# Conditioning products moved from the second router head into the latent turns, and eight expert loads moved with them

## The reference

```python
mod = jax.nn.silu(c) @ w_ada + b_ada            # w_ada: 1024 x 6144
sh1, sc1, ga1, sh2, sc2, ga2 = jnp.split(mod, 6, axis=-1)
h = modulate(rms_norm_2(x, g_attn), sh1, sc1)
x = x + ga1[:, None, :] * hybrid_mixer(h, w_in, b_f, sinks, w_out)
h2 = modulate(rms_norm_2(x, g_mlp), sh2, sc2)
x = x + ga2[:, None, :] * conv_glu_mlp(h2, w_up, conv_w, conv_b, w_down)
return rms_norm_2(x, g_final)
```

## Time and profile before

| | |
|---|---|
| Median of 3 runs | 1623.3 us (1623.09 to 1624.7) |
| The profiled execution | 1624.69 us |
| Its span, first to last instruction | 1622.8 us |
| TensorE, VectorE, ScalarE, POOL busy | 84%, 35%, 16%, 6% of the span |
| Mean granted clock of TensorE | 0.93 |
| Read from HBM | 510.6 MB, 315 GB/s over the span |
| Experts of layer 1: block 0's first product; last block's down products | 786.5 us; 1229.3 to 1233 us |

### The profile page before, as it was taken

How to read it: one execution, slowest core, us unless ns; L and a number is a source line. 1 busy time by engine, 2 the same in 40 slices (tenths; PEclk the granted TensorE clock), 3 DMA queues, 4 the chain that set the end, 5 groups by cost and what they waited for, 6 DMA issues and landing times.

```text
span 1622.8 us, 24320 instructions
## 1 busy us (share of the span) xinstructions
PE 1366.1 (84%) x9358; PEld 827.5 (51%) x9358; DVE 564.2 (35%) x1487; ACT 263.5 (16%) x736; POOL 103.7 (6%) x191
## 2 busy tenths in 40 slices
PE   8999999676776777989998766767767999999998
PEld 4445555343443443555554433433434875888843
DVE  3444543122122222562542221221213143577721
ACT  2144211010010011452111010100101133111100
POOL 1312000000000001210100000000001041000000
PEclk9999999898898898999998888988989979999999
DMA  8868999999999999636999999999999621544400
GB/s 285 310 234 302 370 392 419 421 421 422 422 421 422 422 421 397 225 132 226 380 408 422 420 422 422 422 422 422 422 421 367 231 78 52 195 152 149 141 0 26
DMA packets 117188, 512.76 MB, mean 316 GB/s; under 512 B 11856, under 2 KB 46604, under 8 KB 64888
## 3 DMA queue, kind: packets, MB, share of 16 engines
q1 hardware_dynamic: 115504, 507.56, 79.1%
q0 software_dynamic: 1584, 4.13, 0.8%
q10 hardware_dynamic: 24, 0.02, 0.0%
HBM read 510.61 MB, written 1.07 MB: 315 GB/s over the span
## 4 chain that ended last, share of the span: by engine, by line
PE 34%; DMA 12%; SPq 7%; DVE 2%; issue 1%; ACT 1%; POOL 0%; POOLq 0%; DVEq 0%; ACTq 0%
PE bank L2170 9%; DMA ring<-in_moe_w_up 7%; SPq L1618 6%; PE bank L2185 5%; PE bank L1218 4%; DMA BC<-in_moe_w_up 3%; PE bank L1914 3%; DMA ring<-in_moe_w_down 2%; PE bank L404 2%; PE bank L416 2%; PE bank L1204 1%; PE bank L1233 1%; PE bank L644 1%; PE bank L667 1%; PE bank L501 1%
## 5 line engine op out<-in xcount | busy, mean ns | idle before, releaser
L1218 PE MATMUL bank<-ring,hT 128*32 128x256 f32 (+1 forms) x2912 | 301.4, 462 | 156.2 <-DMA ring<-in_moe_w_up 68.9
L1218 PEld LDWEIGHTS bank<-ring,hT 128*32 128x32 f32 (+1 forms) x2912 | 157.1, 133 | 265.3 <-issue 178.9
L1218 PE MATMUL bank<-BC,hT 128*32 128x256 f32 (+1 forms) x1120 | 164.9, 463 | 48.2 <-DMA ring<-in_moe_w_up 28.2
L1469 DVE TENSOR_SCALAR pT<-pT 128x256 f32<-128x256 f32 x34 | 10.0, 294 | 462.7 <-ACT pT L1585 462.7
L2170 PE MATMUL bank<-hT,ring 128*128 128x256 f32 (+1 forms) x736 | 154.3, 373 | 1.7 <-ACT hT L294 1.7
L2170 PEld LDWEIGHTS bank<-hT,ring 128*128 128x128 f32 x736 | 136.4, 193 | 19.2 <-DVE hT L299 1.9
L501 PE MATMUL bank<-ring,hT 128*128 128x512 f32 (+4 forms) x352 | 123.7, 513 | 9.7 <-DVE hT L297 3.9
L1204 PE MATMUL bank<-A,hn 128*128 128x128 f32 x1088 | 128.1, 276 | 0.0
L1204 PEld LDWEIGHTS bank<-A,hn 128*128 128x128 f32 x1088 | 125.3, 193 | 3.3 <-issue 3.3
L1218 PEld LDWEIGHTS bank<-BC,hT 128*32 128x32 f32 (+1 forms) x1120 | 82.2, 135 | 86.2 <-issue 72.9
L1233 PE MATMUL bank<-ring,gtab 128*32 128x512 f32 (+1 forms) x800 | 123.6, 595 | 2.4 <-DMA ring<-in_moe_w_down 1.9
(11 more groups left out here) (297 smaller groups left out, 1489.7 us busy)
## 6 DMA issues: line engine op xcount, KB each, us to landing
ring<-in_moe_w_down SPq DMA_DIRECT2D x100, 1024.0 KB, 26.3
ring<-in_moe_w_up SPq DMA_DIRECT2D x94, 1024.0 KB, 26.5
ring<-in_moe_w_gate SPq DMA_DIRECT2D x88, 1024.0 KB, 25.3
BC<-in_moe_w_gate SPq DMA_DIRECT2D x36, 1024.0 KB, 25.0
BC<-in_moe_w_up SPq DMA_DIRECT2D x34, 1024.0 KB, 25.9
BC<-in_moe_w_down SPq DMA_DIRECT2D x28, 1024.0 KB, 26.9
ring<-in_w_ada SPq DMA_DIRECT2D x24, 1024.0 KB, 6.4
ring<-in_w_up SPq DMA_DIRECT2D x22, 1024.0 KB, 5.3
```

The lines of the kernel that those rows point to most:

```text
L1218: i = nc.tensor.matmul(GATE[q * cap:(q + 1) * cap, part * FF:(part + 1) * FF], xg[:, c, q * cap:(q + 1) * cap], u[:, c, :], start=(c == 0) ...
```

## The change

`cond3` is planned ahead of `o2` (8 conditioning units, then 4 of the output weights) and uses bank 3. Its products leave the router head: units 0 and 1 stand after `pkv` and ahead of `t4q`, behind a wait for `pkv`'s last copy; units 2 to 4 stand behind fills 1, 3 and 5 of `t4q`, units 5 to 7 behind fills 1, 3 and 5 of `t4k`. ScalarE copies and stores between `t4k` and the attention. Expert units 7 to 14 now follow the conditioning units in their slots, and SyncE loads them right after units 0 and 1; 15 to 18 follow the output weights. In the router head a `KeepWarm` filler issues one product of 512 columns of constants, into bank 1, at each of the eight places; nothing reads it, and its copy and its wait are empty.

```diff
-        def turn_stage(name, ready, jobs, scalar_only=False, fill_ready=None, bank0=4):
+        def turn_stage(name, ready, jobs, scalar_only=False, fill_ready=None, bank0=4, beside=None):
...
                     i.then_inc(turned.sem, 1)
+                    if beside:
+                        beside(pe, f)
...
+        class KeepWarm:
+            def tensor(self, pe, h):
+                nc.tensor.matmul(bank[1][:, :], ident, konst[:, P:P + NB], start=True, stop=True)
+            def bank_read(self, pe):
+                pass
+            def scalar(self, act, h):
+                pass
...
                 for m in range(EXTRA, 18):
-                    load_fixed(m)
+                    if m not in [early for early, _ in slots_free]:
+                        load_fixed(m)
...
-        t4q = l_turn("t4q", q_l, 0, scalar_only=True)
-        t4k = l_turn("t4k", k_l, 1, bank0=6)
+        def condition_first(pe):
+            pe.wait_ge(*pkv.copied(8))
+            cond3.tensor(pe, 0)
+            cond3.tensor(pe, 1)
+
+        def condition(first):
+            def beside(pe, f):
+                if f % 2 and f < 6:
+                    cond3.tensor(pe, first + f // 2)
+            return beside
+        t4q = l_turn("t4q", q_l, 0, scalar_only=True, beside=condition(2))
+        t4k = l_turn("t4k", k_l, 1, bank0=6, beside=condition(5))
...
+        cond3 = Conditioning(2, 3, 8, 3)
         o2 = OutStage(square_units(t["mla_w_out"][0], D, order="(c p)"), add_x)
         a2 = attention_stage("a2", l_turned, [latent_head(h) for h in range(HEADS)], MLA_QK ** -0.5, causal_bias, o2)
-        cond3 = Conditioning(2, 3, 8, 1)
...
         m2 = moe(1, "m2", o2.ready, a2.ready, rows_turned,
-                 [(3, first_half_2), (5, first_half_2), (4, second_half_2), (6, second_half_2)], cond3, lambda pool: conditioning_gpsimd(pool))
+                 [(m, rows_turned) for m in range(7, 15)] +
+                 [(3, first_half_2), (5, first_half_2), (4, second_half_2), (6, second_half_2)], KeepWarm(), lambda pool: conditioning_gpsimd(pool))
...
             t4k.scalar(act)
+            cond3.scalar(act, 7)
             a2.scalar(act)
...
             pkv.tensor(pe)
+            condition_first(pe)
             t4q.tensor(pe)
```

## The result

The changed kernel takes 1626.64 us (median of 20 executions, 1624.46 to 1631.05), the kernel before, timed beside it, 1624.5 us (20 executions, 1619.7 to 1626.75). The ratio is 1.0020, 95% interval 1.0011 to 1.0028: about 3.3 us slower (1.8 to 4.5); the two medians differ by 2.1. That is a small loss, clear of zero, and near the edge of the band of 0.2% within which the prediction had put it.

A forecast was written before the change was run, and what follows sets the result against it. Weight transfers were taken to bound about 880 to 1229 us, engines the time before. Terms +1.7, +0.5 and -0.5 summed to +1.7 us: 1625.0 from the median, 1626.4 from the profiled execution; given as 1625.2, range 1621.5 to 1628.5.

The forecast's parts named there:

- What bounds it: Second layer: engines set the time until about 880 us, then weight transfers; the queue is empty near 787 and 805 us.
- rival A: Expert loads during the attention: the early load pays, up to 19.9 us off, 1603 to 1619 us; chance 0.07.
- The conditioning products: Between the query and key turns: TensorE alone sets the pace, scores start at 712.48 us; +1.7 us.
- rival E: In the turns: a unit costs its lone price of 1.06 us as the array drains; +3.1, 1626.4 us; chance 0.08.
- The row I held against it: Old router head: the next work began 0.88 us after a lone unit, counted against a lone price of 1.06.
- The rule on small tiles: In the turns: less than full overlap of column tiles would make a unit 1.1 us and the term +3.5.
- ScalarE's copy and store: Before the attention's first exponential: it starts 0.54 us later, as does the first turned map; +0.5 us (0 to 0.7).
- The stand-ins: Router head: length kept, but TensorE's clock may change; full clock makes it 1.05 us shorter; counted -0.5 us (-1.05 to 0).
- I count half: Router head: half of the 1.05 us saved at full clock was counted, giving -0.5 us.
- POOL's small loads: Eight small conditioning and bias loads move from 800 us into the idle head; 0 us, bound -0.6.
- Rival C: In the turns: TensorE falls to half clock between 699 and 711 us, costing 1.85 us; 1627.3 us; chance 0.18.
- Rival B: Router head keeps full clock, 1.05 us off, and later falls move too; net +0.5 to +1.2, 1624 us; chance 0.2.

## Why the prediction was right, and where its sum was off

**What bounds it: right.** The byte count said that the queue is empty at 787 and at 805 us. In the changed kernel it stands idle 17 us earlier, and with the loads put back it is empty at 790 us all the same. The early load is worth nothing that can be measured (rival A), shown by the kernel that lacks it.

**The conditioning products: mis-sized, 1.7 us forecast, 3.24 measured.** The step that failed is the sum 8 x 0.88 + 16 x 0.445 = 14.16 us of work in one string. The shape was right: TensorE is the pace from the last copy to the last fill and waits for nobody. The lengths were right too (0.88 in the string of eight, 0.87 a pair). What was missing is a price for each change between the units' column tiles and the whole array: a pair of fills 0.87 among its like and 1.03 ahead of a unit, a unit 0.88 and 1.00 ahead of a pair. From 695.08 to the end of the issue of the last fills, near 710.8, it is 15.7 us, 1.6 more than the sum; with 0.87 a pair it is 1.8 more, 13 changes at about 0.14. A part of it, some 0.05 at each return to the fills, is also paid behind a wait: a pair's row is 1.09 long behind a wait or a unit and 1.04 straight behind the key/value products. That is rival E, to which I gave 0.08. Its +3.1 was the better number for the string, though half of the price lies on the fills and not on the unit. That the array drains at a change was its reason; the runs show the price and not what happens inside. Half of a fill's transposes are 64 columns wide (rotary channels; 32 of the 64 that the trace lists for line 571), and a pair of such fills takes the same 0.87, so not every change of width is dear. The row I held against it was the wrong one: in the earlier trace rows the unit at 785.57 us is followed after 0.88 by gate products that stand in column tiles themselves, so nothing changes there.

**The rule on small tiles.** By the 2.38 times for three column tiles that the Trainium skill states (TensorE: Matmul & The Clock Gate, Why this matters for your kernels), the term was estimated at +3.5. That is near the 3.24, but for another reason, and the trace does not agree with it: the four tiles overlap fully, 7.01 us for eight units, 0.88 each, as one whole-array product of the same columns takes.

**ScalarE's copy and store: 0.5 forecast, 0.18 measured.** The exponential is 0.37 us late; I took the first turned map to be late by the same. TensorE was still in its scores then, so part of the delay was covered. Where unit 7 stands last, the cover is gone, and it is 0.58.

**The stand-ins: -0.5 forecast, +0.07 in this pair of profiles.** The length of the head is not settled by the code alone. At full clock it is 21.0 to 21.2 us with either filler. With one fall it is 21.9, and it was 23.5 in the kernel with late loads. The fall occurred in 3 of 8 heads with the old filler and in 2 of 5 with the stand-ins. Replacing one by the other changed nothing that can be told; with both left out, the one profile has a fall over most of the head, but so has one of the five with stand-ins. "I count half" was a guess, and no run gives the share well enough to say what it should have been.

**POOL's small loads: 0 forecast.** Block 0 and the pause of the queue at block 1 show no gain (18.20 us before, 18.23 after). They were not tested alone.

**The sum.** Terms of +1.7, +0.5 and -0.5 against +3.24, +0.18 and +0.07. The total of +1.7 lay below the measured 3.3, near the interval's lower end of 1.8. The time fell in the range because that was drawn to take in E and C. The sign and the mechanism held; "within 0.2%" as the likeliest band is by the interval open, since 0.2% is its centre. Counted from the last copy, block 0's gates begin 3.5 us later than before, more than the 1 to 2.5 that I had named as a sign of being right. That the forecast of 1625.2 lies only 1.4 us from the measured 1626.64 owes nothing to a better sum: it starts from a median of 1623.3, and the kernel before took 1624.5 beside the changed one. From there E's +3.1 would give 1627.6 and the forecast's +1.7 1626.2; the ratio is nearer E, the difference of the medians nearer the forecast. Rival C did not occur: with units in the turns, no profile has a fall of the clock between 699 and 711 us. The two without (the kernel before and the same with its gap filled) do have one there, 0.50 near 700 us, and their turns take 13.7 us all the same. Rival B's head at full clock came in 3 of the 5 profiles with stand-ins, though not in the changed kernel's own.

## What to carry to other kernels

Before you load something earlier, count the bytes moved up to the next point at which the queue must wait for a result or a slot: if it is empty there already, the early load buys idle time. Work put into another engine's waits is free only while the sum of that engine's work stays under the stage's pace; add up the whole string, then look at which engine sets the pace after the edit. Keep products of one tiling together: a change between column tiles of 32 and the whole array costs about 0.14 us here, a little more than a transpose (0.11).

## What the hardware showed unexpectedly

The change of tiling costs even where the products are tiny: the pair ahead of a unit of 8 columns takes 1.02 us, one ahead of a unit of 512 columns 1.03, one ahead of another pair 0.87. And the same code with the same idle gap of 1.67 us takes 21.0 or 21.9 us from one execution to the next, by whether TensorE's clock (granted 1.00 or 0.50) falls behind it. Without stand-ins the clock had fallen to 0.50 by 774 us, less than a microsecond into the gap of 5.22 us and behind a shorter one of 1.32, and it stayed there over the counts and most of the gather, to 787 us.
